# A mixture-of-experts stage with its first round unrolled, six rotating weight buffers, and gate_up of the next expert ahead of down of this one

## The reference, cut to what matters

```
lg = t @ router_group_w + b;  g_idx = top_1(softmax(lg))          # 4 groups
le = t @ router_expert_w + b; top 2 of the 8 experts of that group # 32 experts
for e in range(32):
    hid = silu(t @ exp_w_gate[e]) * (t @ exp_w_up[e])              # 1024 -> 256
    y = y + comb[:, e] * (hid @ exp_w_down[e])                     # 256 -> 1024
x = LN(alpha*x + gate2 * y)
```

## Time and profile before

| | before |
|---|---|
| device time, 3 runs | 754.37 us median (753.61 to 758.16) |
| span of the profiled execution (its own time; nothing else is recorded for it) | 754.3 us |
| first gate_up starts | 462.54 us |
| last down ends | 708.31 us |
| PE busy over the span | 616.1 us (82%) |
| experts' weights | 96 loads of 1 MiB |

### The profile page before, as it was taken

One profiled execution on the slowest core, in us unless ns is written; L12 is line 12 of the kernel. 1 busy time (PEld: TensorE's weight loads), 2 busy tenths in 40 slices (PEclk: granted clock), 3 DMA queues, 4 the chain that ended last, 5 costly groups with the idle time before them and its releaser, 6 DMA issues.

```text
span 754.3 us, 8345 instructions
## 1 busy us (share of the span) xinstructions
PE 616.1 (82%) x3037; PEld 322.6 (43%) x3037; DVE 248.2 (33%) x497; ACT 122.7 (16%) x238; POOL 133.1 (18%) x190
## 2 busy tenths in 40 slices
PE   1589998999999999999969946988888888778400
PEld 0164345554344455564424544544444444344200
DVE  2322443237553551232217751121111111111146
ACT  0020342210022211150100111021121111111010
POOL 3000000010200000000001213333232323233133
PEclk9699999999999999999989955999999999999855
DMA  9888536137223113074198393869999999999252
GB/s 336 293 255 277 178 126 223 48 124 256 75 79 111 44 69 112 0 217 167 61 399 326 151 396 117 340 236 402 407 406 407 405 404 405 405 404 360 83 186 83
DMA packets 67564, 176.76 MB, mean 234 GB/s; under 512 B 10628, under 2 KB 12580, under 8 KB 67536
## 3 DMA queue, kind: packets, MB, share of 16 engines
q1 hardware_dynamic: 50912, 144.42, 50.2%
q10 hardware_dynamic: 10560, 23.68, 9.1%
q0 software_dynamic: 6064, 8.28, 3.2%
HBM read 175.92 MB, written 11.96 MB: 249 GB/s over the span
## 4 chain that ended last, share of the span: by engine, by line
PE 62%; DMA 12%; SPq 12%; DVE 6%; issue 4%; POOL 2%; ACT 1%; PEldq 1%; POOLq 0%; DVEq 0%; ACTq 0%
PE bank L1400 22%; PE bank L1660 10%; SPq L424 7%; PE bank L1572 6%; PE bank L1585 5%; PE bank L1676 5%; SPq L433 4%; DMA W<-w_ada 4%; DMA W<-exp_w_up 3%; PE bank L1352 2%; DMA Y<-w_ada 2%; PE bank L1530 2%; DMA W<-w_out 2%; PE bank L1548 2%; PE bank L1628 1%
## 5 line engine op out<-in xcount | busy, mean ns | idle before, releaser
L1400 PE MATMUL bank<-W,Y 128*128 128x512 f32 (+1 forms) x432 | 182.0, 574 | 0.0
L1400 PEld LDWEIGHTS bank<-W,Y 128*128 128x128 f32 x432 | 80.1, 190 | 84.9 <-issue 82.6
L1660 PE MATMUL bank<-X,Y 128*64 128x256 f32 x768 | 90.9, 390 | 15.5 <-PE bank L1676 8.1
L606 POOL TENSOR_TENSOR rstd<-ss,cst 128x1 f32<-128x1 f32 (+3 forms) x21 | 25.5, 1214 | 329.4 <-DVE ss L745 329.4
L1660 PEld LDWEIGHTS bank<-X,Y 128*64 128x64 f32 x768 | 57.1, 140 | 58.8 <-issue 37.8
L683 POOL DMA_INDIRECT pair_rows<-PTr,si x32 | 32.6, 1018 | 138.9 <-DVE PTr L1118 138.9
L1676 PE MATMUL bank<-X,abias 128*64 128x512 f32 x192 | 46.5, 605 | 9.8 <-DVE abias L1113 9.8
L1111 DVE TENSOR_TENSOR abias<-abias,bank 128x128 f32<-128x128 f32 x32 | 9.2, 288 | 127.8 <-ACT abias L1317 116.6
L1585 PE MATMUL bank<-W,Y 128*128 128x512 f32 x96 | 44.8, 625 | 6.5 <-DMA W<-w_out 5.8
L1118 DVE COPY PTr<-bank 128x512 f32<-128x512 f32 x32 | 22.1, 691 | 69.9 <-PE bank L1676 69.9
L654 POOL DMA_INDIRECT Y<-h_rows,gi x36 | 36.8, 1023 | 31.4 <-POOL gi L651 23.3
(11 more groups left out here) (204 smaller groups left out, 638.4 us busy)
## 6 DMA issues: line engine op xcount, KB each, us to landing
X<-exp_w_gate SPq DMA_DIRECT2D x24, 1024.0 KB, 7.4
X<-exp_w_up SPq DMA_DIRECT2D x24, 1024.0 KB, 12.4
X<-exp_w_down SPq DMA_DIRECT2D x24, 1024.0 KB, 14.3
W<-w_in SPq DMA_DIRECT2D x8, 2048.0 KB, 8.6
Y<-w_ada ACTq DMA_DIRECT2D x8, 2048.0 KB, 9.5
W<-w_ada SPq DMA_DIRECT2D x4, 2048.0 KB, 10.5
W<-exp_w_gate SPq DMA_DIRECT2D x8, 1024.0 KB, 11.9
W<-exp_w_up SPq DMA_DIRECT2D x7, 1024.0 KB
```

The costliest lines, as they stand in the source:

```text
L606: nc.gpsimd.tensor_tensor(rstd[:, 0:n], ss[:, 0:n], const("mhalf", 0, n), ALU.pow)\
L1400: ins = mm(bank[:, 0:cols], hT[:, i, k, :], w[:, k, :], start=k == 0, stop=k == KT - 1)
L1660: ins = mm(banks[5][hh * 64:hh * 64 + 64, a:b], x_[:, c, h * 64:h * 64 + 64], rhs(hh), start=k == 0 and a == 0, stop=k == KT - 1, skip_gro ...
```

## The change

- The first round over the 32 experts is written out on all engines. The loops remain for the overflow rounds alone, which get semaphores of their own (`O`, `over_...`).
- Expert n uses buffer n % 6. SP issues gate and up of n when gate_up of n-6 is done, and down of n-1 right behind it, when down of n-7 is done. The six loaded before the first expert are now 0 to 5, except that down of expert 5 is left for later: it is issued behind gate and up of expert 6.
- On PE, gate_up of n+1 comes ahead of the transpose and down of n, and `tokens` of n+2 between the transpose and down of n. Gate_up results alternate between bank 5 and bank 2 (`gub`). DVE multiplies for n+1 before it copies the result of n. ACT waits for `hid_ready` of n-1 before silu of n, since `sg` is one buffer.
- POOL hands `gidx` and `sidx` columns to the indirect DMAs directly, without the copies to `gi` and `si` and the waits for them. Scatter of expert m is issued behind gather of m+6.

```diff
@@ SP
-            def round_loads(r):
-                for s in range(NSLOT):
-                    if s not in OWN:
-                        reload(NSLOT + s, s, r * NE + s + 1, r * slot_turns(s) + 1)
-                with sp.Fori(2, TURNS) as it:
-                    for s in range(NSLOT):
-                        reload(it * NSLOT + s, s, r * NE + (it - 1) * NSLOT + s + 1,
-                               r * slot_turns(s) + it - (s in OWN))
+            for n in range(NBUF, NE + 1):
+                if n < NE:
+                    sp.wait_ge(S["gu_full"], n - NBUF + 1)
+                    load_gate_up(sp, n, n % NBUF, ew_in[n % NBUF])
+                m = n - 1
+                if m >= NBUF:
+                    sp.wait_ge(S["y_full"], m - NBUF + 1)
+                load_down(sp, m, m % NBUF, ed_in[m % NBUF])
@@ POOL
+            def gather_rows(n):
+                pool.indirect_dma_start(G[:, n % NSLOT, :], None, h2_d,
+                                        bass.IndirectOffsetOnAxis(ap=gidx[:, n:n + 1], axis=0),
...
+            pool.wait_ge(S["idx_ready"], 1)
+            for n in range(NSLOT):
+                gather_rows(n)
+            for n in range(NSLOT, NE + NSLOT + 2):
+                if n < NE:
+                    pool.wait_ge(S["xTe_full"], n - NSLOT + 1)
+                    gather_rows(n)
+                if n >= NSLOT + 2:
+                    pool.wait_ge(S["y_ready"], n - NSLOT - 1)
+                    scatter_rows(n - NSLOT - 2)
@@ DVE
+            gate_times_up(0)
+            for n in range(NE):
+                dve.wait_ge(S["hT_full"], n + 1)
+                V.tensor_copy(hidT, banks[1][:, 0:P]).then_inc(S["hT_ready"], 1)
+                if n + 1 < NE:
+                    gate_times_up(n + 1)
+                dve.wait_ge(S["y_full"], n + 1)
+                if n >= NSLOT:
+                    dve.wait_ge(scattered[n % NSLOT], (n // NSLOT) * 16)
+                V.tensor_copy(Yo[:, n % NSLOT, :], banks[6][:, :]).then_inc(S["y_ready"], 1)
@@ PE
+            def next_tokens(n):
+                pe.wait_ge(g_in[n % NSLOT], (n // NSLOT + 1) * 16)
+                if n:
+                    pe.wait_ge(S["xTe_ready"], n)
+                tokens(n % NSLOT, S["xTe_full"])
+            def next_gate_up(n):
+                pe.wait_ge(ew_in[n % NBUF], (n // NBUF + 1) * 32)
+                pe.wait_ge(S["xTe_ready"], n + 1)
+                if n >= 2:
+                    pe.wait_ge(S["hid_ready"], n - 1)
+                gate_up(gub[n % 2], xTe[:, n % 2], n % NBUF, S["gu_full"])
+            index_tables(0)
+            next_tokens(0)
+            next_gate_up(0)
+            next_tokens(1)
...
+            for n in range(NE):
+                if n + 1 < NE:
+                    next_gate_up(n + 1)
+                pe.wait_ge(S["hid_ready"], n + 1)
+                if n:
+                    pe.wait_ge(S["hT_ready"], n)
+                tp(banks[1][:, 0:P], hid, ident).then_inc(S["hT_full"], 1)
+                if n + 2 < NE:
+                    next_tokens(n + 2)
+                pe.wait_ge(ed_in[n % NBUF], down_target(n))
+                pe.wait_ge(S["hT_ready"], n + 1)
+                if n:
+                    pe.wait_ge(S["y_ready"], n)
+                down(ebuf[n % NBUF][1], S["y_full"])
```

More of the change, by code:

```diff
@@ L444, in program @@
         TURNS = NE // NSLOT
[L446 to L456, removed]
         def settle(eng):
@@ L686, in turns @@
                             .then_inc(scattered[s], 16)
[L688 to L694, removed]
                 for s in range(NSLOT):
-                    pool.wait_ge(g_in[s], (r + 1) * (TURNS + 1) * 16)
+                    pool.wait_ge(over_g_in[s], r * (TURNS + 1) * 16)
                     settle(pool)
@@ L1102, in experts @@
             def experts(r):
[L1103 to L1107, removed]
+                tables(r)
+                settle(dve)
+                with dve.Fori(0, TURNS) as it:
                     for s in range(NSLOT):
[L1109 to L1114, removed]
-                        settle(dve)
-                        if not first(r, it):
-                            dve.wait_ge(scattered[s], (r * TURNS + it) * 16)
-                        V.tensor_copy(Yo[:, s, :], banks[6][:, :]).then_inc(S["y_ready"], 1)
@@ L1120, in experts @@
[L1120 to L1128, removed]
+                        n = (r - 1) * NE + it * NSLOT + s
+                        dve.wait_ge(O["silu_ready"], n + 1)
+                        V.tensor_tensor(hid, sg, banks[5][:, P:2 * P], ALU.mult).then_inc(O["hid_ready"], 1)
@@ L1315, in experts @@
                         n = it * NSLOT + s
[L1316 to L1321, removed]
+                        act.wait_ge(O["gu_full"], (r - 1) * NE + n + 1)
+                        A_(sg, banks[5][:, 0:P], ACT.Silu).then_inc(O["silu_ready"], 1)
+                        act.wait_ge(O["xTe_full"], (r - 1) * (NE + 1) + n + 2)
+                        tokens((s + 1) % 2, O["xTe_ready"])
             overflow(act, experts)
@@ L1622, in _, with index_tables @@
             main.wait_read(pe, "router")
[L1624 to L1631, removed]
+            def index_tables(r):
                 pe.wait_ge(S["onehot_ready"], r + 1)
@@ L1636, in experts, with tokens, gate_up @@
                 ins.then_inc(S["tables_full"], 1)
-                pe.wait_ge(g_in[0], (r * (TURNS + 1) + 1) * 16)
-                tokens(0)
-                def turns(it):
+            def tokens(b, done):
+                g = G[:, b, :].rearrange("p (q c) -> p q c", c=4)
+                for c in range(4):
+                    ins = tp(banks[0][:, c * P:(c + 1) * P], g[:, :, c], ident)
+                ins.then_inc(done, 1)
+            def gate_up(bank, x_, w, done):
+                wg, wu = ebuf[w][0]
+                for k in range(KT):
+                    h, c = k // 4, k % 4
+                    if w < len(egu):
+                        parts = [(0, 2 * P, lambda hh: egu[w][:, :, k, hh * P:(hh + 1) * P])]
+                    else:
+                        parts = [(0, P, lambda hh: wg[:, k, hh * P:(hh + 1) * P]),
+                                 (P, 2 * P, lambda hh: wu[:, k, hh * P:(hh + 1) * P])]
+                    for a, b, rhs in parts:
+                        for hh in range(2):
+                            ins = mm(bank[hh * 64:hh * 64 + 64, a:b], x_[:, c, h * 64:h * 64 + 64],
+                                     rhs(hh), start=k == 0 and a == 0, stop=k == KT - 1,
+                                     skip_group_check=True)
+                ins.then_inc(done, 1)
@@ new lines, in down @@
+            def down(wd, done):
+                for hh in range(2):
+                    for o in range(2):
+                        ins = mm(banks[6][o * 64:o * 64 + 64, :], hidT[:, hh * 64:hh * 64 + 64],
+                                 wd[hh][:, o * HALF:(o + 1) * HALF], start=hh == 0, stop=hh == 1,
+                                 skip_group_check=True)
+                ins.then_inc(done, 1)
+            def next_tokens(n):
[3 more added lines that the diff above has]
+                tokens(n % NSLOT, S["xTe_full"])
@@ L1640, in turns, with experts @@
+            def experts(r):
+                index_tables(r)
+                pe.wait_ge(over_g_in[0], ((r - 1) * (TURNS + 1) + 1) * 16)
+                tokens(0, O["xTe_full"])
+                with pe.Fori(0, TURNS) as it:
                     for s in range(NSLOT):
                         n = it * NSLOT + s
-                        own = isinstance(it, int) and s in OWN
-                        w = OWN[s] if own else s
-                        x_, (wg, wu), wd = xTe[:, s % 2], ebuf[w][0], ebuf[w][1]
@@ L1670, in turns @@
-                        if own:
-                            pe.wait_ge(ed_in[w], 32 if w == PARTED else 16)
-                        else:
-                            pe.wait_ge(ed_in[s], (r * slot_turns(s) + it + 1 - (s in OWN)) * 16)
-                        for hh in range(2):
-                            for o in range(2):
-                                ins = mm(banks[6][o * 64:o * 64 + 64, :], hidT[:, hh * 64:hh * 64 + 64],
-                                         wd[hh][:, o * HALF:(o + 1) * HALF], start=hh == 0, stop=hh == 1,
-                                         skip_group_check=True)
@@ L1679, in turns @@
-                        ins.then_inc(S["y_full"], 1)
-                        if not own:
-                            pe.wait_ge(S["y_full"], r * NE + n + 1)
-                            pe.nop().then_inc(ew_free[s], 1)
-                turns(0)
-                with pe.Fori(1, TURNS) as it:
-                    turns(it)
-            experts(0)
+                        pe.wait_ge(over_w_in[s], ((r - 1) * TURNS + it + 1) * 32)
+                        pe.wait_ge(O["xTe_ready"], (r - 1) * (NE + 1) + n + 1)
@@ new lines, in experts @@
+                        gate_up(banks[5], xTe[:, s % 2], s, O["gu_full"])
```

(6 more changed lines are left out.)

156 lines of the change are left out of this document (86 added, 70 removed).

## The result

| | before | changed |
|---|---|---|
| device time, median | 755.16 us (4 runs) | 744.40 us (742.98 to 745.41, 4 runs) |
| ratio, 95% interval | | 0.985 (0.982 to 0.987) |
| span of the profiled execution | 754.3 us | 741.1 us (its own time 742.98) |
| first gate_up starts | 462.54 us | 461.04 us |
| last down ends | 708.31 us | 696.66 us |

The kernel became 10.8 us faster, by the ratio's interval 1.3 to 1.8%. The forecast was 744.5.

A forecast was written before the change was run, and what follows sets the result against it. The prediction took the weight stream over DMA to bound the mixture's end, with PE's remaining work behind the last byte. Its sum was 754.3 - 10.4 + 2.7 - 1.1 - 1.0 = 744.5 us, range 740.5 to 750.5.

The forecast's parts named there:

- The hole: Idle DMA time at 485 to 500 us in the weight stream closes with n % 6 buffers: -10.4 us (9 to 11.5).
- One load more: Down of expert 5, no longer loaded before the first expert, adds 1 MiB to the full stream: +2.7 us.
- The start: The first gather, ahead of gate_up of 0, no longer waits for the copy of its index: -1.1 us.
- PE's order: PE's new order matters only behind the last weights, at the end of the mixture: -1.0 us (+1.2 to -3.2).
- PE's pace: PE's time per expert in the mixture falls from 7.39 to 6.9 us (bounds 6.65 and 7.39), alone worth nothing more.
- PARTED and unrolling: Using PARTED five times costs 0; straight code for the experts adds some 10 instruction packets, taken as 0 (0 to 10).
- Rival 1: Unrolled code stalls PE while instruction packets are fetched during the mixture: slower, at 764 us; chance 0.06.
- Behind the last down: From the end of the last down to the end of the kernel nothing changes: 46 us.
- 2 (engines that end apart): A few DMA engines end the weight stream late, so 4 to 10 us come back: say 750 us; chance 0.13.
- 3 (PE's pace stays): PE's period per expert in the mixture stays 7.39 us, giving a span of 749.6 us; chance 0.06.
- 4 (a fuller queue moves more): The weight stream runs at 414 GB/s in place of 405 and ends 4.9 us earlier: 739.6 us; chance 0.03.
- 5 (the SP queue blocked): A wait in the new load order blocks SP's queue, so the change fails to do what it says: 754 us; chance 0.02.

## Why the prediction was right, point by point

**The hole (-10.4).** Right, in mechanism and size. The first issue of the stream came 468.98 - 466.10 = 2.9 us earlier. Up of 31, which now has 1 MiB (2.7 us) more behind it, was there at 687.34 in place of 701.16. So the end of the stream moved by 13.8 - 2.7 = 11.1 us; the terms give 2.9 + 10.4 - 2.7 (one load more) = 10.6. A second count needs no price for a load. Between the first issue of the stream and gate_up of 31 lie the same 77 MiB in both kernels, and it takes 701.28 - 468.98 = 232.3 us before and 687.39 - 466.10 = 221.3 now, 11.0 less for 10.4 of hole. The two runs that bring the old buffers back lose 8.0 and, by the ratios, 8.4 us. Neither has the whole 10.4: the first has a hole of 7.7, the second one of 9.3 and down of 3 loaded ahead, which is worth a load.

**One load more (+2.7).** Right: taking it out again gains 2.6 us.

**The start (-1.1).** Right in the copy, short in the sum. The first gather starts 1.3 us earlier (456.06 against 457.37), of which the copy is 1.1, and gate_up of 0 another 0.2. The remaining 1.4 of the 2.9 to the first freed buffer are the clock. PE's granted clock stood at 0.50 of 2.4 GHz until 468 in the kernel before, and gate_up of 0 took 6.41 us; here it rose to 1.00 by 464, inside this gate_up, which took 5.03. PE was busy with gate_up of 0 in both cases when it rose. The stretches, columns as in the earlier trace rows, before and changed:

```profile
462.50:469.00 6.50, 6.46 (x33) 3.94 (x34) 0.00 (x0) 1.21 (x2) 3.24 (x6) 0.57 0.18 53
462.00:467.00 5.00, 4.75 (x34) 3.05 (x30) 0.29 (x1) 0.69 (x3) 0.42 (x1) 0.82 0.12 37
```

It isn't the change's doing as far as these runs show: the same kernel took 6.42 us in another profile. Why the rise comes early in one execution and late in another is open.

**PE's order (-1.0).** Right that it acts only at the end. Bringing the old order back costs 2.1 us (3.0 by the ratios), within the bounds given (-3.2 to +1.2). It isn't a clean test of the term: in that run gate_up of 31 comes 5.2 us later, as it stands behind down of 30, and what PE does from there on is 2.3 us shorter (7.0 against 9.3). The prediction took this term from the order of PE alone. The runs show that it belongs to a pair: PE's new order pays with the load order of the change, and gains nothing with the old one.

**PE's pace (6.9, bounds 6.65 to 7.39).** Wrong, without a cost. It is 6.08. The step that failed is the lower bound: I added up durations that had been recorded beside waits. In the changed kernel, too, the gate_up that starts behind 0.78 us of waiting, at 467.53, counts 3.67. Back to back, gate_up counts 3.45 and not 3.67, tokens 0.48 and not 0.68, the transpose 0.26 and not 0.34, down 1.89 and not 1.96. PE therefore caught up with the weights at 559 and not near 630, and from there on waited for them at 16 gate_ups, 23.6 us in all. From the first of these to the last an expert takes (687.39 - 561.66) / 15 = 8.4 us, and not 8.1:

```profile
PE bank L1672 <- DMA X<-exp_w_up: 16.4, 11, 2.6
PE bank L1672 <- DMA Y<-exp_w_up: 4.4, 3, 2.0
PE bank L1672 <- DMA W<-exp_w_up: 2.8, 2, 2.4
```

**PARTED and unrolling (0).** Right. The instruction queue has 27 packets and not 18, nine more where ten were expected, and PE is busy 5.00 of 5.00 us in every stretch from 470 to 510. Rival 1 is out.

**Behind the last down (46 us).** Wrong by some 2.5 us: 44.4, 42.9 and 43.0 in three profiles of the changed kernel. PE's branch and gate2's loads were my theory for it, and no time supports it: the runs that moved each of them came out at 743.64 and 744.34 us. The profiles say where the time lies. Before, the chain waits 8.71 us for the loads of pair_rows, which are issued 2.2 us behind those of gate2 (715.25 against 713.06). In three profiles of the changed kernel it waits 6.4 to 6.5 us, and 4.2 to 6.9 us lie between the two. With the wait ahead of PE's branch it waits 7.87 us, with 1.2 us between them, and the end takes 44.1. So the nearness of gate2's loads fits some 2 of the 3 us in the profiles. As the time of that run isn't longer, it isn't shown, and what shortened the end stays open.

**The total.** The profiled execution of the changed kernel has a span of 741.1, 3.4 under the sum of 744.5: 1.8 at the start, 1.4 of it the clock, and 1.6 behind the last down. Between the two the sum was right: it had the last down end 8.7 us earlier by the hole, the added load and PE's order (10.4 - 2.7 + 1.0), and the profiles have 11.0 less the 2.2 that PE takes longer behind the landing of up of 31, 8.8. From profile to profile the gain is 13.2 us where the sum had 9.8, and by the medians 10.8. A program's time is 1.7 to 1.9 us over its span (742.98 against 741.1), and I had set the two equal. And the profiled execution was a quick one (742.98 of 742.98 to 745.41). So that 744.5 hit the median of 744.4 to 0.1 us is luck: these cancel.

**The other rivals.** 2 (engines that end apart): the taper is there, 0.75 and 0.49 in 680 to 690, but it took nothing of the gain, by the 11.0 us for a hole of 10.4. 3 (PE's pace stays) is out. 4 (a fuller queue moves more): out, 400 to 407 GB/s. 5 (the SP queue blocked) is out: expert 8 is issued at 477.36. The Trainium skill's section "Instruction fetch mechanics" ("Runtime: NRT & Kernel Launch") says that a taken branch to code further away stalls until it is fetched, and that crossing from one block of straight code to the next is mostly hidden. The trace here agrees with both in what it can show: 3.3 us for PE's branch over the overflow rounds, no gap at nine more packets. That the 3.3 us are a fetch no run here shows.

## What to carry to other kernels

When a stream of loads sets the end, count idle DMA time from the first moment at which a buffer is free, and look at which load the issuing queue is waiting to send. Here closing a hole gained its whole length, moving a load into idle time ahead gained that load's length, and a faster consumer gained only at the very end. The order of the last loads and the order of the consumer's last steps have to be chosen together. A period added up from recorded durations is too long for work that will run back to back, and a prediction of a median should add what lies around the span.

## What the runs showed of the hardware

- PE's granted clock fell to 0.88 of 2.4 GHz in 560 to 600 in the changed kernel, where it was 1.00 in the same stretch before. PE had waited 2.59 us for weights ahead of gate_up at 561.66. The clock then stood at 1.00 until 562, at 0.50 from 563 to 566 and at 1.00 again from 567, with PE busy throughout, and this gate_up took 5.36 us in place of 3.67. The stream lost nothing by it, its share stayed at 1.03.
- In the changed kernel PE's sequencer ran the load, the compare and the branch of the overflow test at 694.9 to 697.9, while the last down ran from 694.72 to 696.67. Without a wait between them, control code isn't behind the matmuls.
- In the kernel before, the branch over the overflow rounds took 3325 ns on PE's queue and 50 to 63 ns on SP, ACT, DVE and POOL.
- The fastest kernels of this study are those with down of 5 ahead: 741.07 us, and 740.74 with gate2 early as well, 0.982 of the kernel before. What is left in the stream is its taper (a share of 1.01, 0.64, 0.39 and 0.02 in the stretches of 5 us from 675 to 695, with down of 5 ahead) and the 37 us between PE's pace and the weights'.
